# Output projection of an attention layer: its first five pieces multiplied inside the loop over attention pairs

## The reference, cut to what matters

```
a_x = _blocked_attention(q_x, k_all, v_all)                   # latent queries, 512 keys
y_x = concat([_fourier_mix(u_x), a_x]) @ w_out
a_c = _attend(q_c, k_c, v_c)                                  # context queries, 256 context keys
y_c = concat([_fourier_mix(u_c), a_c]) @ w_out
x   = x + mx[2] * _rms_norm(y_x, ...)                         # then the dense SwiGLU, the SSD layer, the experts
```

## Time and profile before

| | |
|---|---|
| median of 3 runs | 1859.52 us (1858.22 to 1859.78) |
| the profiled execution: time, span | 1858.6 us, 1856.3 us |
| busy: PE, DVE, ACT, POOL | 97%, 61%, 49%, 3% of the span |
| context pairs, S(12) to S(19) | 169.23 to 193.36 us |
| first matmul of the projection | 204.59 us |
| mean granted clock of TensorE | 0.995 of full |

### The profile page before, as it was taken

One profiled execution on the slowest core, in us unless ns is written; L12 is line 12 of the kernel. 1 busy time (PEld: TensorE's weight loads), 2 busy tenths in 40 slices (PEclk: granted clock), 3 DMA queues, 4 the chain that ended last, 5 costly groups with the idle time before them and its releaser, 6 DMA issues.

```text
span 1856.3 us, 25612 instructions
## 1 busy us (share of the span) xinstructions
PE 1796.1 (97%) x10135; PEld 1316.2 (71%) x10136; DVE 1131.1 (61%) x1485; ACT 916.9 (49%) x1436; POOL 54.4 (3%) x49
## 2 busy tenths in 40 slices
PE   6989999999999999899999999999999999999997
PEld 5976788888888877687887566666666566655563
DVE  3266466765657797687867565555555555555644
ACT  3335572222246646587756465554454445444443
POOL 1000000000000121100200000000000000000000
PEclk9999999999999999999999999999999999999999
DMA  9456215665455532022259999999999999999995
GB/s 355 147 202 254 91 46 182 201 204 192 151 183 196 160 104 69 27 88 68 92 203 344 393 394 406 409 412 414 409 407 411 412 413 410 408 412 412 413 406 236
DMA packets 182457, 498.21 MB, mean 268 GB/s; under 512 B 10347, under 2 KB 62907, under 8 KB 167995
## 3 DMA queue, kind: packets, MB, share of 16 engines
q1 hardware_dynamic: 181760, 495.93, 70.7%
q10 hardware_dynamic: 571, 0.57, 0.1%
HBM read 495.42 MB, written 1.05 MB: 267 GB/s over the span
## 4 chain that ended last, share of the span: by engine, by line
PE 78%; DVE 8%; ACT 5%; DMA 4%; SPq 3%; issue 2%; ACTq 0%; POOL 0%; DVEq 0%; POOLq 0%
PE bank L974 12%; PE bank L975 11%; PE bank L976 11%; PE bank L1664 9%; PE bank L1656 4%; PE bank L1239 4%; PE bank L1240 4%; PE bank L1241 4%; DMA raw<-in_moe_gu_w_dram 2%; DVE ar L3028 2%; SPq L854 2%; PE bank L1339 1%; PE bank L1340 1%; PE bank L1341 1%; SPq L849 1%
## 5 line engine op out<-in xcount | busy, mean ns | idle before, releaser
L2668 DVE TENSOR_TENSOR lo<-raw,hi 128x1024 fp32r<-128x1024 f32 x182 | 216.6, 1222 | 171.4 <-ACT hi L1958 169.6
L2649 DVE TENSOR_TENSOR lo<-raw,hi 128x1024 fp32r<-128x1024 f32 x172 | 212.0, 1238 | 146.0 <-ACT hi L1938 144.5
L1938 ACT ACTIVATE hi<-raw 128x1024 fp32r<-128x1024 f32 x156 | 164.6, 1059 | 260.0 <-PE bank L1241 172.6
L1958 ACT ACTIVATE hi<-raw 128x1024 fp32r<-128x1024 f32 x182 | 186.4, 1056 | 148.5 <-DMA raw<-in_moe_gu_w_dram 58.2
L974 PE MATMUL bank<-hi,xg_t 128*128 128x512 f32 x448 | 182.4, 407 | 2.5 <-DVE xg_t L3218 1.2
L975 PE MATMUL bank<-lo,xg_t 128*128 128x512 f32 x448 | 175.2, 391 | 0.0
L976 PE MATMUL bank<-hi,xg_t 128*128 128x512 f32 x448 | 174.9, 390 | 0.0
L2668 DVE TENSOR_TENSOR lo<-ar,hi 128x1024 fp32r<-128x1024 f32 x94 | 112.1, 1222 | 90.9 <-ACT hi L1958 89.7
L974 PE MATMUL bank<-hi,hth 128*128 128x512 f32 x400 | 160.0, 400 | 3.0 <-DVE lo L2668 3.0
L975 PE MATMUL bank<-lo,hth 128*128 128x512 f32 x400 | 156.0, 390 | 0.0
L976 PE MATMUL bank<-hi,htl 128*128 128x512 f32 x400 | 155.8, 390 | 0.0
(11 more groups left out here) (400 smaller groups left out, 3288.0 us busy)
## 6 DMA issues: line engine op xcount, KB each, us to landing
raw<-in_moe_gu_w_dram SPq DMA_DIRECT2D x126, 1024.0 KB, 16.5
raw<-in_moe_down_w_dram SPq DMA_DIRECT2D x60, 1024.0 KB, 16.8
ar<-in_moe_gu_w_dram SPq DMA_DIRECT2D x59, 1024.0 KB, 18.2
out_slot<-in_moe_gu_w_dram SPq DMA_DIRECT2D x39, 1024.0 KB, 15.9
ar<-in_moe_down_w_dram SPq DMA_DIRECT2D x33, 1024.0 KB, 15.7
raw<-in_ada_w_dram SPq DMA_DIRECT2D x14, 2048.0 KB, 9.1
raw<-in_ffn_gu_w_dram SPq DMA_DIRECT2D x22, 1024.0 KB, 5.1
raw<-in_ffn_down_w_dram SPq DMA_DIRECT2D x22, 1024.0 KB, 4.9
```

The costliest lines, as they stand in the source:

```text
L1938: A_(hi[:, p % SPL, :], raw[:, slot(u), (p % 2) * PIECE:(p % 2 + 1) * PIECE], ACT.Copy).then_inc(hi_ready, 1)
L1958: A_(hi[:, q % SPL, :], m_raw(i)[:, (q % 2) * PIECE:(q % 2 + 1) * PIECE], ACT.Copy).then_inc(m_hi, 1)
L2649: TT(lo[:, p % SPL, :], raw[:, u, h * PIECE:(h + 1) * PIECE], hi[:, p % SPL, :].bitcast(F32), ALU.subtract).then_inc(done, 1)
L2668: TT(lo[:, q % SPL, :], src[:, (q % 2) * PIECE:(q % 2 + 1) * PIECE], hi[:, q % SPL, :].bitcast(F32), ALU.subtract).then_inc(m_lo, 1)
```

## The change

Pieces 0 to 4 of the projection move into the loop. Each is cut in two parts of 6 matmuls, one for each latent block (`mix_out_part(i, b2)`). Pieces 0 to 3 stand in j = 12 to 19, one part for each iteration, between S and PV, in the place of the fills; the parts of piece 4 stand in j = 20 and 21 behind PV. The six fills behind the loop are gone as well. The splits of the pieces move with them: `hi_to` and `lo_to` are called at the end of iterations 11, 13, 15, 17, 19, 20 and 21, one piece each (`mixout_pieces`). On ACT the call stands behind the copies of pair j - 1 and ahead of stage 3; on DVE behind stage 3. The banks of sums and of the gates change, because the old ones are in use by attention in the loop. Pieces 5 to 15 follow the loop, with `grow_(0)` and `grow_(1)` behind piece 5 instead of 1 and `grow_(2)` and `grow_(3)` behind piece 8 instead of 5; ACT's `grow_out` and the first evacuation move to fit.

```
+        def mixout_bank(ps, half, b2):
+            return bank[(6, 0 if ps == 0 else 4)[half] + b2]
+        def mixout_pieces(j):
+            return max(0, (j - CTX_PAIR) // 2 + 1) if j < N_PAIRS else j - N_PAIRS + 5
...
+            def mix_out_part(i, b2):
...
+                if b2 == 0:
+                    pe.wait_ge(lo_ready, p + 1)
...
+                    if i == 12:
+                        pe.wait_ge(grow_ready, 4)
+                a = (2 * ps + b2) * P
+                for t in range(2):
+                    k = 2 * q + t
+                    m = tok3(mixout_bank(ps, half, b2)[:, :], xh[:, k, a:a + P], xl[:, k, a:a + P],
+                             *wpart(p, t, 512), first=(k == 0), last=(k == KC - 1))
+                if b2 == 1:
+                    m.then_inc(piece_used, 1)
...
# PE
-                if j >= CTX_PAIR:
-                    fill(bank[7][:, 256:512], 1 if j % 4 else 2 if j < N_PAIRS else 3)
+                if CTX_PAIR <= j < N_PAIRS:
+                    mix_out_part((j - CTX_PAIR) // 2, (j - CTX_PAIR) % 2)
                 if ("att" in [k for k, _ in pair_of(j - 2)]):
                     att_pv([i for _, i in pair_of(j - 2)])
+                if j >= N_PAIRS:
+                    mix_out_part(4, j - N_PAIRS)
...
-            fill(bank[7][:, 256:512], 6)
-            pe.wait_ge(at_ol, 4)
-            pe.wait_ge(dft_lo, 8)
-            pe.wait_ge(ada_done, N_RAW_ADA)
...
+            for i in range(5, N_MIXOUT):
                 for b2 in range(2):
+                    mix_out_part(i, b2)
+                if i == 5:
                     pe.wait_ge(mod_ready, 5)
+                    pe.wait_ge(at_ol, 4)
                     grow_(0)
                     grow_(1)
-                if i == 5:
+                if i == 8:
                     pe.wait_ge(grow_ready, 2)
                     grow_(2)
                     grow_(3)
# ACT, in the loop over j
+                if j >= CTX_PAIR - 1:
+                    hi_to(P_MIXOUT + mixout_pieces(j + 1))
                 for k, i in pair_of(j - 2):
                     stage_3(k, i)
-            hi_to(2 * S_MIXOUT + SPL)
...
-                if i == 2:
+                if i == 5:
+                    mix_evac(0, 0)
+                if i == 6:
                     grow_out(0)
-                if i == 3:
                     grow_out(1)
-                    mix_evac(0, 0)
-                if i in (5, 6):
-                    grow_out(i - 3)
+                if i in (9, 10):
+                    grow_out(i - 7)
# DVE, in the loop over j
                 for k, i in pair_of(j - 2):
                     stage_3(k, i)
-            lo_to(2 * S_MIXOUT + SPL)
+                if j >= CTX_PAIR - 1:
+                    lo_to(P_MIXOUT + mixout_pieces(j + 1))
```

More of the change, by code:

```diff
@@ L548, in grow_bank @@
         def grow_bank(r, k):
-            return bank[4 + 2 * (r % 2) + k]
+            return bank[(4 + 2 * (r % 2) if r >= 4 else 2 + 2 * (r % 2)) + k]
+        def mixout_bank(ps, half, b2):
+            return bank[(6, 0 if ps == 0 else 4)[half] + b2]
+        def mixout_pieces(j):
+            return max(0, (j - CTX_PAIR) // 2 + 1) if j < N_PAIRS else j - N_PAIRS + 5
         def norms(n):
@@ L1156, in att_pv @@
                             m.then_inc(at_pv, 1)
+            def mix_out_part(i, b2):
+                ps, r = divmod(i, N_MIXOUT // 2)
+                half, q = divmod(r, 4)
+                p = P_MIXOUT + i
+                if b2 == 0:
+                    pe.wait_ge(lo_ready, p + 1)
+                    if i == 0:
+                        pe.wait_ge(dft_lo, 8)
+                        pe.wait_ge(ada_done, N_RAW_ADA)
+                    if i == 2:
+                        pe.wait_ge(at_ol, 2)
+                    if i == 4:
+                        pe.wait_ge(at_exp, 32)
+                    if i == 8:
+                        pe.wait_ge(at_ol, 4)
+                        pe.wait_ge(lin_evac, LIN_MIXOUT + 2)
+                    if i == 12:
[7 more added lines that the diff above has]
+                    m.then_inc(piece_used, 1)
             for j in range(N_PAIRS + 2):
@@ L1190, in grow_ @@
                 m.then_inc(grow_t, 1)
[L1192 to L1199, removed]
-                for b2 in range(2):
[L1201 to L1210, removed]
+            for i in range(5, N_MIXOUT):
+                for b2 in range(2):
+                    mix_out_part(i, b2)
+                if i == 5:
                     pe.wait_ge(mod_ready, 5)
+                    pe.wait_ge(at_ol, 4)
                     grow_(0)
                     grow_(1)
-                if i == 5:
+                if i == 8:
                     pe.wait_ge(grow_ready, 2)
@@ L2119, in mix_evac @@
                 for b2 in range(2):
-                    A_(y[:, 2 * ps + b2, half * 512:(half + 1) * 512], bank[4 * ps + 2 * b2 + half][:, :], ACT.Copy
+                    A_(y[:, 2 * ps + b2, half * 512:(half + 1) * 512], mixout_bank(ps, half, b2)[:, :], ACT.Copy
                        ).then_inc(lin_evac, 1)
-            for i in range(N_MIXOUT):
+            for i in range(5, N_MIXOUT):
                 hi_to(P_MIXOUT + i + 1 + SPL)
-                if i == 2:
+                if i == 5:
+                    mix_evac(0, 0)
+                if i == 6:
                     grow_out(0)
-                if i == 3:
                     grow_out(1)
-                    mix_evac(0, 0)
-                if i in (5, 6):
-                    grow_out(i - 3)
+                if i in (9, 10):
+                    grow_out(i - 7)
                 if i == 7:
```

## The result

| | |
|---|---|
| after, median of 17 runs | 1864.13 us (1859.77 to 1865.64) |
| before, median of 17 runs | 1857.97 us (1856.25 to 1861.05) |
| ratio | 1.0028, 95% interval 1.0022 to 1.0035: +5.2 us |
| forecast | 1860 us, 1854.5 to 1864.5, "no change that can be told" |
| profiled execution: time, span, mean granted clock | 1864.13 us, 1861.8 us, 0.990 |

The change made the kernel slower by 0.28% (5.2 us by the ratio, 6.2 us by the two medians). The number lies in the range, near its upper end; the likeliest case of the forecast, no change, was not what came. The forecast of 1860 us stood on a median of before of 1859.52 us from 3 runs, so it said +0.5 us; over 17 runs before is 1.5 us lower.

What follows compares the result with a forecast made beforehand. PE, busy 97% of the span, was taken as the bound. Profiled 1858.6 us, less 2.7 for order, plus 3.4 for two clock falls, gave 1859.3; the median stands 0.9 higher: 1860 us, range 1854.5 to 1864.5.

Steps and rivals of the forecast that it cites:

- the likeliest case of the forecast: Case (a), whole kernel: waits as forecast, one or two clock falls, 1858.4 to 1860.1 us; chance 0.53.
- All five waits: PE idle ahead of the first part in j = 12, 14, 16, 18, 20: 2.6, 3.4, 2.2, 3.4 and 2.3 us.
- the order alone: Loop to the first gates: PE's new order, without new clock falls, saves 218.4 - 215.7 = 2.7 us.
- 218.4 us: When piece 5 would start in before, counted with the two gates moved behind it; the change was put at 215.7.
- I take two falls at 1.7 us: +3.4: Loop: two of the new PE waits are followed by half clock, costing 1.7 us each, 3.4 us in all.
- My bound for the short waits: Waits of 2.2 to 2.6 us were judged nearer the 2.11 us wait ahead of 114.15, after which the clock stayed 1.00.
- Rival (c): Loop: the clock falls behind each of the five waits, +8.5 us, 1865.3 us; chance 0.19.
- (b): Rival, loop: the clock holds because dense parts stand on either side of each wait, 1856.8 us; chance 0.22.
- (d): Rival, loop: the splits are hidden and PE alone sets it at 3.2 us a pair, 1841 us; chance 0.06.
- Costs set at nothing: Splits on ACT and DVE, SP's weight loads, late gates and `mod_ready` cost nothing; `norm_t` changes by -0.2 to 0 us.
- sets nothing here: Loop, DVE: normalisation and maximum queued behind `lo` finish some 1.7 us later, covered by PE's part and PV (2 us).

Runs made afterwards that it cites:

- e1: The changed kernel with 4, 6, 4, 6 and 2 fills on PE ahead of its five waits for the splits; ratio 0.9989 to before, 1857.05 us.
- e7: e6 with the part also moved behind T(j-1) on PE, as in e2; ratio 0.9914 to before, 1842.94 us.
- e3: The changed kernel with each split one iteration earlier and behind stage 3 on ACT and DVE; ratio 1.0031 to before, 1864.24 us.
- e5: The kernel before with only the splits of pieces 0 to 3 placed as in the change, PE untouched; ratio 1.0060, 1868.98 us.
- e6: The changed kernel with `hi` and `lo` of a piece in different iterations, both behind stage 3; ratio 0.9937 to before, 1847.01 us.
- e8: The kernel before with splits of pieces 0 to 3 in the loop, `hi` and `lo` in different iterations, behind stage 3; ratio 0.9999, 1858.87 us.
- e2: The changed kernel with the part moved behind T(j-1) on PE, splits left in place; ratio 0.9981 to before, 1854.81 us.
- e4: The changed kernel with the edits of both e2 and e3; ratio 0.9996 to before, 1857.56 us.

## Why the prediction came out as it did

**Order, right.** All five waits are there, released by DVE's `lo`, within 0.3 us of the forecast except the last (1.54 instead of 2.3). Where no fall disturbs, in e1, the double iterations from S(13) take 10.5, 9.0 and 10.0 us; I had 10.3, 8.7 and 9.8. The order was forecast to give 2.7 us, and e1 gives 2.0. But the sum called this "the order alone", and it is not: 218.4 us is a time of before with its two falls, 3.4 us, in it. Without them the same count has the order lose 0.7 us. The traces agree: from S(12) to `norm_t`, with 1.7 us taken off for each fall, before has about 76.8 us and the changed kernel 77.3. The move of five pieces won nothing in order: by the counts of the prediction 25.5 us left (pieces 13.8, fills 11.7), and 14 us of parts and the 12.5 us of waits came.

**The clock, mis-sized: the step "I take two falls at 1.7 us: +3.4".** The price was right (3.4 us at half clock), the count was not: four came in the loop, +6.8. So -2.7 + 6.8 = +4.1, and the stretch from S(12) to `norm_t` measured +4.0. Fall against fall, that is two more than before has in its loop, 3.4 us, and 0.5 us of order. My bound for the short waits was one row, the 2.11 us ahead of 114.15 behind which the clock stayed up. In the profiled execution of after the same wait, 2.11 us at the same place, was followed by a fall (the rows at 114 and 116 above); and the wait of 2.10 us ahead of 196.11 and that of 1.54 ahead of 218.13 were too, while the first, 2.48 us, was not. The clock falls behind such a wait in some executions and not in others, so one row could not bound it.

**Rival (c)**, five falls at 1865.3, was thus the nearest in mechanism, one fall too many; it was to decide from four falls on. I had given it 0.19. That the measured time lies in the range is luck in part: on the median of before over 17 runs, 1.5 us lower, the same sum gives about 1858.5 us and a range that ends at about 1863, below 1864.13. (b), the clock holds, is out for this kernel, and is what e1 shows once the waits are filled. (d), PE alone sets the loop, was rightly excluded for this order; e7 has the order in which it holds.

**Costs set at nothing.** `grow_out(3)` and `mod_ready` did not stop PE: the gates start at 227.26, right behind piece 5. `norm_t` came without its former wait of 0.23 us. Not weighed: the fall at 115, 1.7 us, and the longer time at half clock near 760, both outside the change.

**The reason given for "no cost" of DVE's queue was incomplete.** I wrote that the normalisation behind `lo` "sets nothing here", which is true while PE stands for `lo` itself. It hid the ring, and with it the cure: I took PE's wait for the fault, and e3, which removes just that wait, won nothing.

**Open.** Why a fall lasts 6.8 us instead of 3.4, in e5's loop and near 760 us in the changed kernel; and what part of the changed kernel's 5.2 us the falls outside the loop have (at 115 us it is 1.7 of the 5.5 us between the two profiled spans), since they are not counted over the 17 runs.

## What to carry to other kernels

When two engines with fixed orders each do a step of the other's loop, a helper that one makes and the other finishes in the same iteration ties them into a ring; put the two halves in different iterations before anything else is tuned. When a gain is added up from times of before, look for falls of the clock in them and take them out first, or they are booked as a gain of the new order. When a wait is removed and the time stays, follow the engines round once and add up what lies between two starts of the same instruction. And where constant matmuls are replaced by real ones that must wait, price the wait twice, once as time and once as a fall of the clock, even if it is only 2 us.

## What the runs showed of the hardware

The same wait of PE, 2.11 us at 114 us, was followed by the full clock in the profiled execution of before and by 3.4 us at half clock in those of the changed kernel and of e1, e3, e6, e7 and e8, and by the full clock again in e2, e4 and e5 (waits of 2.10 to 2.12 us in all of them). The work of these kernels is the same up to there. The same holds for the short ones: behind 0.36 and 0.68 us of waiting in j = 14 and 15 the clock fell in the profile of before and stayed up in that of e8. So a fall behind a wait of this size comes in one profiled execution and not in the next, worth 1.7 us each time, and single profiles of such kernels differ by that. Its length differs as well: the wait of 3.19 us near 760 us has 3.4 us at half clock around it in the profile of before and 6.8 us in that of the changed kernel, the same work in both.
